# One-hot keys built on other engines, and up blocks loaded into eight slots instead of four

## The reference, cut to what matters

```python
def expert_block(args):
    xb, eb, gb = args      # tokens, their 128 experts each, and the gates of those
    hid = jax.nn.gelu(jnp.einsum('cd,ckd->ck', xb, w_down[eb]).astype(jnp.float32))
    return jnp.einsum('ck,ckd->cd', (gb * hid).astype(xb.dtype), w_up[eb])
```

## Time and profile before

| | |
|---|---|
| median of 3 runs | 1669.45 us (1667.72 to 1673.82) |
| profiled execution, its own time | 1670.48 us |
| its span in the trace | 1668.7 us |
| busy in the span | PE 1608.9 us, DVE 1173.1, ACT 838.8, POOL 670.5 |
| transfers | 471.58 MB, 283 GB/s over the span |
| granted clock of TensorE | 0.995 of full speed |

### The profile page before, as it was taken

The page is one execution under the profiler, slowest core; times in us unless marked ns, Lnnn a source line. Parts: engine busy times, 40 slices in busy tenths (PEclk is TensorE's granted clock), DMA queues, the critical chain, the costliest instruction groups (busy, mean ns, idle before and its releaser), DMA issues.

```text
span 1668.7 us, 29335 instructions
## 1 busy us (share of the span) xinstructions
PE 1608.9 (96%) x9192; PEld 1437.0 (86%) x9192; DVE 1173.1 (70%) x3336; ACT 838.8 (50%) x1827; POOL 670.5 (40%) x568
## 2 busy tenths in 40 slices
PE   7989999999999999999999899999999999999997
PEld 6779999999998878787877899999999988777775
DVE  0721969568885889888823249793888758898886
ACT  5654231267762555555556533214776445555554
POOL 6565022056662243333067720222667504333330
PEclk9999999999999999999999999999999999999999
DMA  7344689889999899999865556997999989999994
GB/s 276 116 135 140 197 288 366 270 258 332 332 326 357 289 340 345 333 356 345 272 224 161 145 151 204 362 342 226 326 326 325 362 284 343 345 345 343 339 335 143
DMA packets 130393, 471.58 MB, mean 283 GB/s; under 512 B 14960, under 2 KB 15216, under 8 KB 129904
## 3 DMA queue, kind: packets, MB, share of 16 engines
q1 hardware_dynamic: 88816, 319.25, 55.8%
q0 software_dynamic: 41472, 151.01, 25.8%
HBM read 469.16 MB, written 1.05 MB: 282 GB/s over the span
## 4 chain that ended last, share of the span: by engine, by line
PE 78%; DMA 12%; DVE 3%; ACT 3%; issue 2%; POOL 1%; SPq 0%; DVEq 0%; ACTq 0%; POOLq 0%
PE ps L792 77%; DMA raw<-in_wu 6%; DMA raw<-in_wd 5%; ACT w_hi L504 1%; DMA raw<-in_wm 1%; DVE w_lo L1440 1%; POOL w_lo L421 1%; PE ps L800 1%; ACT arena L494 1%; DVE ps L1478 1%; DVE hT_lo L1507 0%; ACT L483 0%; ACT arena L553 0%; DVE total L1155 0%; DVE xs L1200 0%
## 5 line engine op out<-in xcount | busy, mean ns | idle before, releaser
L792 PE MATMUL ps<-arena,raw 128*128 128x176 f32 x4096 | 636.4, 314 | 19.8 <-DMA raw<-in_wd 10.3
L792 PEld LDWEIGHTS ps<-arena,raw 128*128 128x128 f32 x4096 | 611.7, 190 | 30.4 <-DMA raw<-in_wd 17.0
L504 ACT ACTIVATE w_hi<-raw 128x1024 fp32r<-128x1024 f32 x336 | 355.1, 1060 | 350.2 <-DMA raw<-in_wu 248.8
L792 PE MATMUL ps<-w_hi,hT_lo 128*128 128x512 f32 x1728 | 464.8, 398 | 6.2 <-DVE hT_lo L1507 4.2
L792 PEld LDWEIGHTS ps<-w_hi,hT_lo 128*128 128x128 f32 x1728 | 325.9, 192 | 94.7 <-DVE hT_lo L1507 26.8
L1440 DVE TENSOR_TENSOR w_lo<-raw,w_hi 128x1024 fp32r<-128x1024 f32 x256 | 312.9, 1222 | 91.2 <-ACT w_hi L504 55.6
L434 POOL DMA_INDIRECT arena<-in_wu,ret x128 | 195.9, 1531 | 390.2 <-DVE ps L1478 300.2
L792 PE MATMUL ps<-w_lo,hT_lo 128*128 128x512 f32 x1024 | 279.0, 393 | 0.0
L434 POOL DMA_INDIRECT arena<-in_rows,ret x160 | 158.3, 990 | 292.6 <-ACT ret L685 145.8
L421 POOL TENSOR_TENSOR w_lo<-raw,w_hi 128x1024 fp32r<-128x1024 f32 x80 | 193.2, 2423 | 119.1 <-ACT w_hi L504 69.6
L792 PEld LDWEIGHTS ps<-w_lo,hT_lo 128*128 128x128 f32 x1024 | 195.3, 191 | 41.9
(11 more groups left out here) (137 smaller groups left out, 1410.9 us busy)
## 6 DMA issues: line engine op xcount, KB each, us to landing
raw<-in_wd SPq DMA_DIRECT2D x256, 512.0 KB
raw<-in_wu SPq DMA_DIRECT2D x256, 512.0 KB
raw<-in_wm SPq DMA_DIRECT2D x80, 512.0 KB
arena<-in_rows,ret POOLq DMA_INDIRECT x160
arena<-in_subk SPq DMA_DIRECT2D x2, 1024.0 KB, 10.3
arena<-in_wu,ret POOLq DMA_INDIRECT x128
xs<-in_x SPq DMA_DIRECT2D x2, 512.0 KB, 5.5
arena<-in_poolm SPq DMA_DIRECT2D x1, 1024.0 KB, 8.4
```

The lines of the kernel that those rows point to most:

```text
L504: nc.scalar.activation(whs[:, s], raw[:, s, :], ACT.Copy).then_inc(whi_done, 1)
L792: return nc.tensor.matmul(out, lhsT, rhs, start=start, stop=stop, skip_group_check=shared)
```

## The change

Four things change.

1. First one-hots are finished with their gates in one operation with two operands per partition (`is_equal`, then `mult`): three of the four tokens of a group on POOL (`POOL_TOK = TOK - 1`), the fourth on DVE, as 128x128 from the iota in PSUM. Each waits for `g_mm` as before.
2. Second one-hots are all on ACT: four Abs, and one Relu of 128x512. ACT no longer touches `oh1g` and no longer waits for DVE's compare.
3. Up blocks have eight slots (`UP_RAW`): two in the ring's region (the halfway tokens' rows, and the ring's fifth slot), the four of `raw`, and two where the tokens' transposed `hT` was. Up block b now waits for the low part of block b - 8. Blocks 0 and 1 wait for dots (`row_used`) alone, 2 to 5 for down blocks 124 to 127, 6 and 7 for all down blocks.
4. The w_up gathers use four ring slots instead of five (`UP_RING`). The halfway tokens' gate product has a semaphore of its own, for which POOL waits at group 44.

```diff
-POOL_TOK = TOK // 2
+POOL_TOK = TOK - 1
...
+        slot = q % RING if q < ROWS else (q - ROWS) % UP_RING
...
+        up_raw = [at(HB_AT, DM), at(HB_AT - DM, DM), *(raw[:, s, :] for s in range(RAW)),
+                  at(HT_AT, DM), at(HT_AT + DM, DM)]
...
-                        sp.wait_ge(wlo_dve, l * BLOCKS - RAW + 1 + s)
+                        sp.wait_ge(wlo_dve, l * BLOCKS - UP_RAW + 2 + s + 1)
...
-                for s in range(RAW):
-                    sp.wait_ge(w_used, l * LAYER + UP_FROM - RAW + 1 + s)
-                    sp.dma_start(raw[:, s, :], wu_d[l, s]).then_inc(raw_full[s], 16)
-
-                def load_up(b, s):
-                    load(wu_d, b, wlo_dve, l * BLOCKS + b - RAW + 1, s)
+                sp.wait_ge(row_used, l * GATHERS + EARLY)
+                load_up(0, 0)
+                sp.wait_ge(row_used, l * GATHERS + ROWS)
+                load_up(1, 1)
+                for j in raw_slots:
+                    sp.wait_ge(w_used, l * LAYER + UP_FROM - RAW + j - 1)
+                    load_up(j, j)
+                for j in (6, 7):
+                    sp.wait_ge(w_used, l * LAYER + UP_FROM)
+                    load_up(j, j)
+
+                def load_up_again(b, j):
+                    sp.wait_ge(wlo_dve, l * BLOCKS + b - UP_RAW + 1)
+                    load_up(b, j)
...
-                def build_second(g):
+                def build_first(g):
                     if g > 1:
                         pool.wait_ge(g_mm, g - 1 + l * TGROUPS)
+                    if g == FULL_GROUPS:
+                        pool.wait_ge(halfway_gated, l + 1)
                     for k in range(POOL_TOK):
                         t = token_of(g) + k
-                        nc.gpsimd.tensor_scalar(oh2[:, g % 2, k, :], iota[:, :], i2T[:, t:t + 1], None,
-                                                ALU.is_equal).then_inc(oh2_done, 1)
+                        nc.gpsimd.tensor_scalar(oh1g[:, g % 2, k, :], iota[:, :], i1T[:, t:t + 1], gT[:, t:t + 1],
+                                                ALU.is_equal, ALU.mult).then_inc(oh1_pool, 1)
...
-                    for k in range(POOL_TOK, TOK):
+                    for k in range(TOK):
                         t = token_of(g) + k
                         nc.scalar.activation(oh2[:, g % 2, k, :], iota[:, :], ACT.Abs, scale=-1.0,
                                              bias=i2T[:, t:t + 1]).then_inc(oh2_far, 1)
-                    act.wait_ge(oh1_equal, g + 1 + l * TGROUPS)
-                    for k in range(TOK):
-                        t = token_of(g) + k
-                        nc.scalar.activation(oh1g[:, g % 2, k, :], oh1g[:, g % 2, k, :], ACT.Copy,
-                                             scale=gT[:, t:t + 1]).then_inc(oh1_done, 1)
...
-                    keys = i1T[:, token_of(g):token_of(g) + TOK].unsqueeze(2).to_broadcast([P, TOK, P])
-                    nc.vector.tensor_tensor(oh1g[:, g % 2], numbers3, keys, ALU.is_equal).then_inc(oh1_equal, 1)
+                    t = token_of(g) + POOL_TOK
+                    nc.vector.tensor_scalar(oh1g[:, g % 2, POOL_TOK, :], numbers, i1T[:, t:t + 1], gT[:, t:t + 1],
+                                            ALU.is_equal, ALU.mult).then_inc(oh1_dve, 1)
```

More of the change, by code:

```diff
@@ L62 @@
 RING = 5
+UP_RING = 4
+UP_RAW = 8
 ROWS = PICKS + HALFWAY
@@ L106, in token_of, with ring_uses @@
     return FULL_FROM + g * TOK if g < FULL_GROUPS else SPARSE + (g - FULL_GROUPS) * TOK
+def ring_uses():
+    filled, last, uses = [0] * RING, [None] * RING, []
+    for n in range(LAYERS * GATHERS):
+        q = n % GATHERS
+        slot = q % RING if q < ROWS else (q - ROWS) % UP_RING
+        uses.append((slot, filled[slot], last[slot]))
+        filled[slot] += 1
+        last[slot] = n
+    return uses
 def axpys_after(b):
@@ L288, in build_trunk @@
         raw_full = [sem(f"raw_full{s}") for s in range(RAW)]
+        up_full = {j: sem(f"up_full{j}") for j in (0, 1, 6, 7)}
         out_stored = sem("out_stored")
@@ L325, in build_trunk @@
         ghhi_done, ghlo_done = sem("ghhi_done"), sem("ghlo_done")
-        oh1_equal, oh1_done, oh2_done = sem("oh1_equal"), sem("oh1_done"), sem("oh2_done")
+        oh1_pool, oh1_dve, oh2_done, halfway_gated = (
+            sem("oh1_pool"), sem("oh1_dve"), sem("oh2_done"), sem("halfway_gated"))
         g_mm, gmul_done = sem("g_mm"), sem("gmul_done")
-        ids_split, oh2_far, oh2_act = sem("ids_split"), sem("oh2_far"), sem("oh2_act")
+        ids_split, oh2_far = sem("ids_split"), sem("oh2_far")
         halfway_rows_psum, halfway_rows_sb = sem("halfway_rows_psum"), sem("halfway_rows_sb")
@@ L333, in build_trunk, with blocks, up_arrival @@
         dve_step = sem("dve_step")
[L335 to L339, removed]
+        def blocks(eng, body, first, last, slots=RAW):
+            with eng.Fori(first // slots, last // slots) as i:
+                for j in range(slots):
+                    body(i * slots + j, j)
+        raw_slots = range(2, 2 + RAW)
+        up_fills = BLOCKS // UP_RAW
+        fills = SPLIT // RAW + up_fills
+        def up_arrival(b, j, l):
+            if j in raw_slots:
+                return raw_full[j - 2], (b - j) * (16 // UP_RAW) + 16 + (l * fills + SPLIT // RAW) * 16
+            return up_full[j], (b - j) * (16 // UP_RAW) + 16 + l * up_fills * 16
+        uses = ring_uses()
         block = ctx.enter_context(nc.Block())
@@ L391, in _, with load_up @@
                        RAW, BLOCKS)
-                for s in range(RAW):
-                    sp.wait_ge(w_used, l * LAYER + UP_FROM - RAW + 1 + s)
-                    sp.dma_start(raw[:, s, :], wu_d[l, s]).then_inc(raw_full[s], 16)
-                def load_up(b, s):
-                    load(wu_d, b, wlo_dve, l * BLOCKS + b - RAW + 1, s)
-                blocks(sp, load_up, RAW, BLOCKS)
+                def load_up(b, j):
+                    sp.dma_start(up_raw[j], wu_d[l, bass.ds(b, 1)].rearrange("b p n -> p (b n)")
+                                 ).then_inc(up_arrival(0, j, l)[0], 16)
+                sp.wait_ge(row_used, l * GATHERS + EARLY)
[11 more added lines that the diff above has]
+                    load_up(b, j)
+                blocks(sp, load_up_again, UP_RAW, BLOCKS, UP_RAW)
                 if l + 1 == LAYERS:
@@ L424, in gather @@
                 def gather(q):
[L425 to L428, removed]
+                    s, _, last = uses[q + l * GATHERS]
+                    if last is not None:
+                        pool.wait_ge(row_used, last + 1)
                     table = rows_d if q < ROWS else wu_d.rearrange("l b p n -> (l b p) n")
@@ L458, in _ @@
                 for g in range(TGROUPS):
-                    build_second(g)
+                    build_first(g)
                     if g > 2:
@@ L497, in norm_stats, with high_part @@
                 nc.scalar.activation(std[:, :], total[:, :], ACT.Sqrt).then_inc(std_done, 1)
-            def high_part(n, s, first=False):
-                act.wait_ge(raw_full[s], (n - s) * (16 // RAW) + 16)
+            def high_part(n, s, first=False, less=0):
+                act.wait_ge(raw_full[s], (n - s) * (16 // RAW) + 16 - less)
                 if not first:
@@ L504, in high_part, with up_loads_short @@
                 nc.scalar.activation(whs[:, s], raw[:, s, :], ACT.Copy).then_inc(whi_done, 1)
+            def up_loads_short(l):
+                return l * (LAYER // RAW - fills) * 16
             def high_parts(first, last):
-                blocks(act, high_part, first, last)
+                blocks(act, lambda n, s: high_part(n, s, less=up_loads_short(first // LAYER)), first, last)
             def split_chunks(ready, base, bank, scale, chunks=range(DC)):
@@ L529, in high @@
                 def high(b):
-                    high_part(b + l * LAYER, b % RAW)
+                    high_part(b + l * LAYER, b % RAW, less=up_loads_short(l))
                 high(4)
@@ L711, in scale_first @@
                                              bias=i2T[:, t:t + 1]).then_inc(oh2_far, 1)
-                    act.wait_ge(oh1_equal, g + 1 + l * TGROUPS)
-                    for k in range(TOK):
-                        t = token_of(g) + k
-                        nc.scalar.activation(oh1g[:, g % 2, k, :], oh1g[:, g % 2, k, :], ACT.Copy,
-                                             scale=gT[:, t:t + 1]).then_inc(oh1_done, 1)
-                    act.wait_ge(oh2_far, (g + 1 + l * TGROUPS) * (TOK - POOL_TOK))
-                    near_key = oh2[:, g % 2, POOL_TOK:TOK, :]
-                    nc.scalar.activation(near_key, near_key, ACT.Relu, scale=-1.0, bias=1.0).then_inc(oh2_act, 1)
+                    act.wait_ge(oh2_far, (g + 1 + l * TGROUPS) * TOK)
+                    nc.scalar.activation(oh2[:, g % 2], oh2[:, g % 2], ACT.Relu, scale=-1.0,
+                                         bias=1.0).then_inc(oh2_done, 1)
                 bb = ret[:, BEST_AT:BEST_AT + TILES * P]
@@ L747, in _, with up_high, up @@
```

(40 more changed lines are left out.)

7 lines of the change are left out of this document (3 added, 4 removed).

## The result

The change made the kernel slower, by about 0.5%: 1679.97 us (median of 9) against 1673.12 us of the kernel before (median of 9), a ratio of 1.0047 with a 95% interval of 1.0025 to 1.0069. The forecast was 1648 us, so the sign was wrong. The profiled execution's span grew from 1668.7 to 1679.6 us, by 10.9.

What follows compares the result with a forecast made beforehand. PE bounds the kernel, slowed by four load slots in the up stage and waits in the gate stretch. -16.6 - 1.2 - 3.5 + 0 = -21.3 us gives 1648 us; range 1642 to 1692.

Steps and rivals of the forecast that it cites:

- Eight slots: Up stage: eight load slots in place of four regain 8.3 of 8.8 us a layer, -16.6 us in all.
- The rival of an up stage that does not gain: Up stage: transfers, not slots, set the 2.39 us block pace; about 1665 us, chance 0.12 by rate or gathers.
- Before block 0: PE's idle time just before the first up block: earlier loads save 1.2 of 1.62 us.
- Ring of four: Up stage: four ring slots leave a w_up gather 16.2 us from slot free to use; cost nothing.
- The rival of late gathers: Up stage: gathers wait behind deeper load queues, DVE waits for rows; 1665 us, chance 0.12 shared with the rate.
- ACT: Gate stretch: four Abs and one Relu, 1.9 us and a gelu in a 3.27 us group; gain or loss nothing.
- VectorE's operation: Gate stretch: DVE's one-hot takes 0.25 us, not 0.60, shortening ten waits after two dots by 0.35 us: -3.5 us.
- POOL: Gate stretch: three one-hots of p us each, 3p + 1.39 us a group; p taken as 0.66, loss zero.
- The line of loss: Gate stretch: beyond p = 0.67, POOL's one-hot duration, PE loses 264 us per us of p in all.
- POOL becomes the bound: Gate stretch rival: POOL sets the pace and the kernel ends slower; strong binding chance 0.21, milder 0.12.
- p = 0.77: POOL's one-hot duration if a second operand costs another 0.16 us; a loss of 26 us.
- p = 0.695: POOL's one-hot duration if the second operand costs the skill's estimated 0.085 us; a loss of 7 us.

Runs made afterwards that it cites:

- three slots: Three ring slots for w_up gathers, on the change with two first one-hots on POOL and two on VectorE: 1654.71 us, up stages 297.07 and 297.14 us.
- Plain compares: The change with POOL's three one-hots as compares with one operand and one function, gates left out of three tokens of four: 1651.23 us, ratio 0.9888.
- the slots alone: The change without its new one-hots (eight load slots, four ring slots), against the kernel before: 1655.8 us, ratio 0.9906.
- the one-hots alone: The new one-hots in the kernel before, with four load slots and five ring slots: 1699.11 us, ratio 1.0178.

## Why the prediction was wrong, point by point

- **Eight slots**: right. -8.3 us a layer was taken, -8.0 measured (-8.4 alone). The rate of the transfers did not bind: 358 GB/s at a share of 0.96, and PE is busy 50.00 of 50 us. The rival of an up stage that does not gain is refuted. The limit of about 358 GB/s that the Trainium skill ("DMA: Bandwidth & Descriptors", "Bandwidth") sets against it did not bind: the window from 1400 to 1450 us of the kernel after moved 361 GB/s. The same section gives the figure as the share of each of two cores that stream together, and here one core runs.
- **Before block 0**: PE's idle time there was 1.62 us in both layers together and is 0.94 us; 0.7 where 1.2 was taken.
- **Ring of four**: right, cost nothing; shown by three slots, which cost nothing either. The rival of late gathers is refuted with it: no wait of VectorE for rows in the up stage after.
- **ACT**: right, nothing. For the gates at 369.65 its Relu ends at 366.12, 3.5 us ahead.
- **VectorE's operation**: 0.25 us taken, 0.32 measured from start to start (0.41 us long). The wait after two dots fell from 0.72 to 0.44 us, where POOL did not hide it: ten of them are 2.8 us where 3.5 was taken. Plain compares take 2 us a layer less than the slots alone (190.5 against 192.6), but only 1.4 of it is this; the rest lies behind the gates, where PE waited less, mostly for loads. In the change itself the shorter wait shows once a layer, and later POOL's lateness took it back.
- **POOL: this step failed**, in one line, "I take p = 0.66, near the old row, since it is the same form of instruction". The form was not the same in what costs time: the second function adds 0.10 us and the second operand 0.09. The rest of the sum held within about 1 us a term. The line of loss, 264 us per us of p over 0.67, gives 264 x (0.787 - 0.67) = 31 us at the measured p, and -21.3 + 31 = +9.6 us; the span grew by 10.9. That the two lie so close is partly luck: from the first gates to the up stage the corrected sum has 31 - 3.5 - 1.2 = 26 us and 24 were measured, and 3 us elsewhere stood in no term. The rival "POOL becomes the bound" had its turning point at p = 0.75 to 0.78 and is what happened, and it was given 0.21.
- The rows already held the warning: 0.16 us that a compare with one operand costs over a two-tensor operation by the fit, worked out as p = 0.77, was set aside for a guess. That 0.77 came so near is luck all the same: it gave the whole 0.16 us to a second operand, which costs 0.09, and nothing to the second function, which costs 0.10. The Trainium skill's figure for a small read ("GPSIMD Engine Reference", "Performance pitfalls for Q7 kernels"), 0.085 us by estimate, lies close to the 88 ns that the second operand took here; that they are the same thing no run shows. The estimate p = 0.695 from it left out the second function.
- **Not accounted for**: the time between the first layer's up stage and the second's gates was 315.6 us before, 317.7 after, and 315.1 to 318.5 in the other kernels without order; and the very end, from the last up matmul, takes 1.5 us longer in the kernels with eight slots (15.3 us or a little more, against 13.9 before and in the one-hots alone). Up to the store of the result both need the same 8.8 us, so the 1.5 us come after it. SP's wait for PE's sequencer at the end of the program is 1.7 us where it was 0.2; what lies behind it was not tried.
- **The high end of the range**: 264 x (0.83 - 0.67) = 42 us puts it at 1690, not 1692; it changes nothing.

## What to carry to other kernels

When an engine is left with little idle time in a repeated group, write its stream as a sum and find the duration at which it becomes the bound before choosing a value for an unknown operation; if the turning point lies inside the unknown's bounds, the forecast is a coin toss and its chances should say so. Merging two operations into one is not free on an engine whose cost per instruction grows with its operands and functions. Two edits that go together should be costed and run apart: here one was worth -0.9% and the other +1.8%. And what is queued ahead of the operation that another engine waits for is worth its whole duration: moving `hidden` up gave 3.3 us a layer for no work.

## What the runs showed of the hardware that was not expected

On GpSimd a `tensor_scalar` of 128x128 float32 takes 608 ns with one operand per partition and one function, 712 ns with a second function by a constant, 800 ns with a second operand as well. On VectorE the two-function form of 128x128 from PSUM takes 0.41 us, 0.32 from start to start, against 0.69 and 0.60 for one compare of 128x512, so four times the elements cost less than twice the time. With eight load slots the transfers of the kernel after moved 353 to 361 GB/s in full windows of 50 us at a share of 0.96 to 0.97, and more slots did not slow the gathers enough to matter: down to three ring slots no row came late.
